# Gate columns projected first and row sums in two rounded parts, in the mixer of a two-layer trunk

## The chip, the core and the metric

One core of a Trainium2 chip runs the whole program. Its engines are TensorE (PE in the profile; PEld is its weight loading), VectorE (DVE), ScalarE (ACT), GpSimd (POOL) and SyncE (SP), each with its own instruction queue, ordered among each other by semaphores. The metric is the device time of one execution in microseconds, as the median of several runs.

## The reference, cut to what matters

Each of two layers adds a token mixer, a cross-attention and an expert retrieval to the residual stream. Only the front of the mixer is touched.

```python
def hybrid_mixer(h, w_in, conv_w, a_log, dt_bias, ...):     # h: 512 tokens x 1024
    proj = h @ w_in                                         # 1024 x 3600 columns
    gdn_qkv, gdn_gate, gdn_a, gdn_b, fox_qkv, fox_f = split(proj)
    gq, gk, gv = split(silu(causal_depthwise_conv(gdn_qkv, conv_w)))
    gq, gk = l2_norm(gq), l2_norm(gk)                       # 4 heads x 128
    log_alpha = -exp(a_log) * softplus(gdn_a + dt_bias)     # 4 columns
    beta = sigmoid(gdn_b)                                   # 4 columns
    o_gdn = gated_delta_rule(gq, gk, gv, log_alpha, beta)   # g = cumsum of log_alpha in chunks of 64
    fq, fk, fv = split(fox_qkv)
    fq, fk = rms_norm(fq), rms_norm(fk)                     # 8 heads x 64
    log_f = log_sigmoid(fox_f + fox_f_bias)                 # 8 columns
    o_fox = attention(fq, fk, fv, bias c_t - c_s, c = cumsum(log_f))
```

## The kernel before

Work is staged: at the end of a stage every compute engine drains and waits for the three others (`stage_end`). All times below are of layer 1; layer 2 runs the same code.

**Projection (S_PROJ).** A weight group is 512 columns of weights, 8 chunks of 128 rows of the contraction. For a product in full precision each operand is split into a rounded part (type fp32r) and the rest: ScalarE copies the rounded part (`w_hi` L868, `x_hi` L871), GpSimd subtracts for the weights (`w_lo` L1600), VectorE for the activations (`x_lo` L1226), and TensorE adds three products of parts (L451 to L453). A chunk of a group is so 4 tiles times 3 = 12 matmuls of 512 columns. `w_hi` and `w_lo` are rings of 4 chunks: ScalarE writes chunk c + 4 when TensorE has used chunk c, and writes the first 4 chunks (EARLY) of the next group before it stores the results of this one. Seven groups of 512 columns run (six for q, k, v, gate and the fox q and k, in a loop over pairs; one for fox v), then an eighth that has the 16 gate columns alone (16 moving columns, 96 matmuls). ScalarE stores each tile to `raw` (L905), VectorE convolves 12 of them (L1254, L1257), and at the end ScalarE applies SiLU to the gate (L914) and to the convolved tiles (L917).

**Norm factors (S_PREP).** VectorE forms 16 squares (L1215) into two buffers, TensorE sums each over its rows in plain fp32 (L493: `row_sums`), ScalarE makes the factors with Ln and Exp (L859, L861), TensorE spreads each row of factors over 128 partitions (L503: `spread_rows`), VectorE multiplies (L1291, L1293). The chain of the gate columns (L1263 to L1285 on VectorE, L921 to L925 on ScalarE) runs ahead of the squares.

**Cumulative sums (S_GATES).** TensorE forms them as columns and as rows (L534 to L542), ScalarE stores them and sends the fox rows to DRAM (`crow_dram`, L936); TensorE spreads the four other rows (L549) and ScalarE stores them to `gb` (L944).

Then S_KQ starts (L1302 on VectorE, L560 on TensorE). Much later, at the start of S_ONORM, one DMA reads `crow_dram` back to all partitions (`crow_all`, L974), for use in S_FOX (L1400).

## Time and profile before

| | us |
|---|---|
| median of 3 runs (4617.79 to 4626.66) | 4624.86 |
| the profiled execution | 4638.87 |
| its span | 4637.1 |
| layer 1: seven full groups of the projection, 29.2 to 191.4 | 162.2 |
| layer 1: from the end of the seventh group to the start of S_KQ, 191.4 to 296.9 | 105.5 |

The page gives the busy time of each engine, then the span in 40 slices, then DMA, then the chain of work that ended last. TensorE is 93% busy over the span, so a slice is worth looking at only where its digit or its clock (PEclk, tenths of full speed) is low. Each slice is 116 us. PEclk is 6 to 8 in slices 2 to 7 and in those that answer to them in layer 2, and 9 in nearly all others; the front of the mixer lies in slices 1 to 3.

### The profile page before, as it was taken

The numbers are of one execution on the slowest core, as the hardware profiler recorded it, in microseconds if no ns is written. First come the engines' busy times: TensorE is split into PE (matmuls) and PEld (weight loads), VectorE is DVE, ScalarE is ACT, GpSimd is POOL, SyncE is SP. The second block draws the span as 40 slices with busy tenths as digits, with TensorE's granted clock in tenths as the row PEclk, the third lists the DMA queues.
The fourth block names the chain that finished last, engine by engine and source line by source line (L and its number), as shares of the span: only waits on it lengthen the run. The fifth ranks groups of instructions, "written<-read, shape, count | busy, mean of one in ns | idle before, by whom it ended". The sixth has DMA issues, their size and how long they took to land.

```text
span 4637.1 us, 65551 instructions
## 1 busy us (share of the span) xinstructions
PE 4297.2 (93%) x20162; PEld 3507.6 (76%) x20162; DVE 2701.9 (58%) x5793; ACT 1534.5 (33%) x2429; POOL 1967.2 (42%) x1210
## 2 busy tenths in 40 slices
PE   7879888899999998999888798888999999989998
PEld 6648666688888887888776586666888888878886
DVE  5043523247586867888751426232566777778886
ACT  3311434333333333333333114343333232333333
POOL 4221132334343436777442311423343434367773
PEclk9867688999999999999998667889999999999999
DMA  3200021224353537999621001212243535379996
GB/s 121 87 1 1 35 76 63 91 79 144 125 200 122 204 119 286 343 336 341 228 110 73 1 1 46 81 55 84 93 143 120 205 119 207 135 284 341 336 335 226
DMA packets 218467, 695.21 MB, mean 150 GB/s; under 512 B 28224, under 2 KB 60992, under 8 KB 210128
## 3 DMA queue, kind: packets, MB, share of 16 engines
q1 hardware_dynamic: 132656, 448.94, 27.7%
q0 software_dynamic: 45888, 138.58, 7.8%
q10 hardware_dynamic: 39776, 105.86, 6.1%
q8 instruction: 76, 1.25, 0.1%
q14 instruction: 71, 0.58, 0.0%
HBM read 590.49 MB, written 102.79 MB: 150 GB/s over the span
## 4 chain that ended last, share of the span: by engine, by line
PE 64%; issue 23%; POOL 6%; DVE 3%; ACT 2%; DVEq 1%; ACTq 1%; POOLq 1%; DMA 0%
PE PS L451 16%; PE PS L452 16%; PE PS L453 16%; POOL u_lo L1663 6%; PE PS L503 2%; PE PS L812 1%; PE PS L493 1%; PE PS L632 1%; PE PS L633 1%; PE PS L597 1%; PE PS L583 1%; PE PS L727 1%; PE PS L627 1%; PE PS L622 1%; PE PS L660 1%
## 5 line engine op out<-in xcount | busy, mean ns | idle before, releaser
L1663 POOL TENSOR_TENSOR u_lo<-u_raw,u_hi 128x1024 fp32r<-128x1024 f32 x256 | 625.9, 2445 | 970.1 <-ACT u_hi L1084 970.1
L451 PE MATMUL PS<-h_hi,u_hi 128*128 128x512 f32 x2048 | 806.1, 394 | 3.0 <-POOL u_lo L1663 1.9
L452 PE MATMUL PS<-h_lo,u_hi 128*128 128x512 f32 x2048 | 797.3, 389 | 0.0
L453 PE MATMUL PS<-h_hi,u_lo 128*128 128x512 f32 x2048 | 797.2, 389 | 0.0
L1600 POOL TENSOR_TENSOR w_lo<-wring,w_hi 128x512 fp32r<-128x512 f32 (+1 forms) x352 | 459.6, 1310 | 621.7 <-ACT w_hi L868 618.7
L451 PE MATMUL PS<-v_hi,g_hi 128*128 128x512 f32 x1536 | 602.9, 392 | 24.4 <-DVE v_lo L1561 12.7
L452 PE MATMUL PS<-v_lo,g_hi 128*128 128x512 f32 x1536 | 601.7, 392 | 0.0
L453 PE MATMUL PS<-v_hi,g_lo 128*128 128x512 f32 x1536 | 601.4, 392 | 0.0
L1084 ACT ACTIVATE u_hi<-u_raw 128x1024 fp32r<-128x1024 f32 x256 | 271.0, 1060 | 948.4 <-PE PS L453 890.9
L1165 ACT ACTIVATE v_hi<-v_raw 128x1024 fp32r<-128x1024 f32 x256 | 271.5, 1061 | 575.5 <-PE PS L453 545.5
L1681 POOL DMA_INDIRECT v_row<-in_expert_v,row_index x256 | 382.3, 1493 | 167.9 <-DVE X L1567 110.3
L451 PEld LDWEIGHTS PS<-h_hi,u_hi 128*128 128x128 f32 x2048 | 384.9, 188 | 81.7 <-issue 5.1
L453 PEld LDWEIGHTS PS<-h_hi,u_lo 128*128 128x128 f32 x2048 | 384.4, 188 | 80.0
L452 PEld LDWEIGHTS PS<-h_lo,u_hi 128*128 128x128 f32 x2048 | 384.9, 188 | 76.2
L1675 POOL DMA_INDIRECT act<-acts_dram,act_index x256 | 394.2, 1540 | 108.0 <-issue 77.4
L868 ACT ACTIVATE w_hi<-wring 128x512 fp32r<-128x512 f32 (+1 forms) x352 | 215.2, 611 | 546.3 <-PE PS L453 479.1
L1567 DVE SCALAR_TENSOR_TENSOR X<-v_row,w,X 128x1024 f32<-128x1024 f32 x256 | 329.0, 1285 | 66.4 <-issue 50.9
L451 PEld LDWEIGHTS PS<-v_hi,g_hi 128*128 128x128 f32 x1536 | 291.1, 190 | 86.9 <-issue 26.3
L1561 DVE TENSOR_TENSOR v_lo<-v_raw,v_hi 128x1024 fp32r<-128x1024 f32 x256 | 313.4, 1224 | 72.2 <-ACT v_hi L1165 71.9
L452 PEld LDWEIGHTS PS<-v_lo,g_hi 128*128 128x128 f32 x1536 | 291.2, 190 | 60.5
L453 PEld LDWEIGHTS PS<-v_hi,g_lo 128*128 128x128 f32 x1536 | 290.8, 189 | 60.9
L1530 DVE TENSOR_SCALAR hot<-cst,pickT 128x128 f32<-128x128 f32 x384 | 221.9, 578 | 77.4 <-PE PS L812 47.4
(299 smaller groups left out, 7249.1 us busy)
## 6 DMA issues: line engine op xcount, KB each, us to landing
u_raw<-in_expert_u SPq DMA_DIRECT2D x256, 512.0 KB, 3.5
v_raw<-in_expert_v SPq DMA_DIRECT2D x256, 512.0 KB
wring<-in_weights SPq DMA_DIRECT2D x44, 2048.0 KB, 7.9
acts_dram<-act_ring ACTq DMA_DIRECT2D x256, 256.0 KB, 2.0
saved<-acts_dram SPq DMA_DIRECT2D x64, 768.0 KB
gates_dram<-gstage ACTq DMA_DIRECT2D x16, 2048.0 KB, 7.5
gates<-gates_dram SPq DMA_DIRECT2D x64, 512.0 KB
crow_all<-crow_dram ACTq DMA_DIRECT2D x2, 2048.0 KB, 8.4
```

The costliest lines, as they stand in the source:

```text
L451: mm(bank_ap, a_hi, b_hi, start=first, stop=False)
L452: mm(bank_ap, a_hi, b_lo, start=False, stop=False)
L453: return mm(bank_ap, a_lo, b_hi, start=False, stop=final)
L1084: fn(u_hi[:, slot, :], u_raw[:, slot, :], ACT.Copy).then_inc(uhi_ready, 1)
L1165: fn(v_hi[:, k % QUAD, :], v_raw[:, k % QUAD, :], ACT.Copy).then_inc(vhi_ready, 1)
L1530: v.tensor_scalar(hot(t, k)[:, 0, es], iota, hi_key, gate_col, ALU.is_equal, ALU.mult)
L1561: v.tensor_tensor(v_lo[:, k % QUAD, :], v_raw[:, k % QUAD, :], v_hi[:, k % QUAD, :].bitcast(f32), ALU.subtract).then_inc(vlo_ready, 1)
L1567: v.scalar_tensor_tensor(X[:, 0, :], v_rows[r][:], w0[:, bass.ds(g * PAIR + k, 1)], X[:, 0, :], ALU.mult, ALU.add).then_inc(macs_done, 1)
L1600: g.tensor_tensor(w_lo[:, c % WCHUNKS, 0:cols], wring[:, s, c, 0:cols], w_hi[:, c % WCHUNKS, 0:cols].bitcast(f32), ALU.subtract).then_inc( ...
L1663: g.tensor_tensor(u_lo[:, slot, :], u_raw[:, slot, :], u_hi[:, slot, :].bitcast(f32), ALU.subtract).then_inc(ulo_ready, 1)
L1675: g.indirect_dma_start(act0[:, k:k + 1], None, acts_by_place, bass.IndirectOffsetOnAxis(act_index[:, k:k + 1], 0)).then_inc(act_gathered[h ...
L1681: g.indirect_dma_start(v_rows[k % GATHERS][:], None, value_rows, bass.IndirectOffsetOnAxis(row_index[:, k:k + 1], 0)).then_inc(row_gathere ...
```

## The change

The stages S_PROJ, S_PREP and S_GATES become one, in this order of groups: first the 16 gate columns (group 0, now with the 16 weight columns stationary and 512 tokens moving), then the six groups of 512 columns (1 to 6), then fox v (group 7). The work of the other two stages is put between and into the groups.

- SyncE loads only the 16 columns for group 0 (pieces of 64 bytes).
- After group 1 TensorE turns the 16 rows into columns; VectorE's and ScalarE's gate chain follows beside groups 2 and 3.
- After group 3 TensorE forms the cumulative sums (4 products in place of 32) and waits until ScalarE has stored them; after group 4 one product turns them to rows, which go to DRAM, and TensorE waits until they have left PSUM.
- `gb` is read back from DRAM by four DMAs on ScalarE's queue, and `crow_all` by four DMAs, one for each 128 tokens, in pieces of 512 bytes instead of 2,048.
- The 16 squares are made twice: ScalarE's Square gives the rounded part, VectorE squares again and subtracts. TensorE sums both parts (32 fp32r matmuls instead of 16 fp32 ones, which the trace shows as two records each), three items behind each chunk of group 7.
- The factors are rounded into two parts as well, held in rows 0 to 23 and 32 to 55 of one tile, so that one fp32r matmul spreads an item.

```diff
+                for p in range(MIX_GROUPS):
+                    q, s = p // 2, p % 2
+                    if p >= 2:
+                        sp.wait_ge(w_free[s], l * N_PAIRS + (q + 1))
+                    if p == 0:
+                        sp.dma_start(wring[:, s, :, 0:16],
+                                     w_layer[PAIR_VS, 1].rearrange("p (c n) -> p c n", n=512)[:, :, 0:16]).then_inc(w_loaded[s], 16)
+                    else:
+                        sp.dma_start(wring[:, s].rearrange("p c n -> p (c n)"), w_layer[(p - 1) // 2, (p - 1) % 2]).then_inc(w_loaded[s], 16)
...
+                def small_product(c, m):
+                    return parts_product(PS[0:16, 7, :], w_hi[:, c % WCHUNKS, 0:16], w_lo[:, c % WCHUNKS, 0:16],
+                                         x_hi[:, c, :], x_lo[:, c, :], c == 0, c == DC - 1)
...
+                def mix_group(p, after_chunk=None):
+                    i0, b0 = 4 * (p - 1), 4 * ((p - 1) % 2)
+                    product = token_tile(0, (x_hi, x_lo), 512) if p == MIX_GROUPS - 1 else channel_tile(b0, (x_hi, x_lo), SEQ)
+                    weight_group(DC * p, 4, product, proj_done, free=lambda m: (raw_stored, i0 + m + 1), after_chunk=after_chunk)
...
+                def cumulative_sums():
+                    pe.wait_ge(gate_cols, 1)
+                    pe.wait_ge(raw_stored, 16)
+                    mm(PS[:, 7, 0:16], tri_chunk, la, start=True, stop=True)
+                    mm(PS[:, 7, 16:32], strict, la, start=True, stop=True)
+                    mm(PS[:, 7, 32:64], tri, lf, start=True, stop=False)
+                    mm(PS[:, 7, 32:64], ones, rinv[:], start=False, stop=True).then_inc(cums_done, 1)
+
+                def sums_to_rows():
+                    pe.wait_ge(cols_ready, 1)
+                    pe.wait_ge(raw_stored, 20)
+                    mm(PS[0:48, 3, 0:P], g_and_c, ident, start=True, stop=True).then_inc(rows_done, 1)
...
+                    pe.wait_ge(sq_hi_ready, i + 1)
+                    mm(PS[0:NROW2, 4, :], lhsT, sq_hi[:, i % 2, :], start=i == 0, stop=False)
+                    pe.wait_ge(sq_ready, i + 1)
+                    mm(PS[0:NROW2, 4, :], lhsT, sq_lo[:, i % 2, :], start=False, stop=i == N_QK - 1).then_inc(ss_done, 1)
+
+                def qk_row_sums(c):
+                    for i in range(3 * c, min(3 * c + 3, N_QK)):
+                        qk_row_sum(i)
+
+                weight_group(0, 1, small_product, small_done, x_chunk=lambda c: XP_MIX + c + 1)
+                mix_group(1)
+                small_to_columns()
+                pe.wait_ge(small_stored, 1)
+                mix_group(2)
+                mix_group(3)
+                cumulative_sums()
+                pe.wait_ge(cols_ready, 1)
+                mix_group(4)
+                sums_to_rows()
+                pe.wait_ge(rows_stored, 1)
+                mix_group(5)
+                mix_group(6)
+                mix_group(7, after_chunk=qk_row_sums)
+                pe.wait_ge(rs_ready, 1)
+                for i in range(N_QK):
+                    if i >= 4:
+                        pe.wait_ge(normed, i - 3)
+                    lhsT = sel_r[0:NROW2, i:i + 1].to_broadcast([NROW2, P]) if i < 8 else sel_pairs[0:NROW2, i - 8, :]
+                    mm(PS[:, 4 + i % 4, :], lhsT, rs_parts[0:NROW2, :], start=True, stop=True).then_inc(bc_done, 1)
```

```diff
+                def soft_exps():
+                    act.wait_ge(softarg, 1)
+                    fn(soft[:, :, :], soft[:, :, :], ACT.Exp, bias=zero_col, scale=-1.0)
+                    fn(nmax[:, 0:GH], par[:, PC["a_log"]:PC["a_log"] + GH], ACT.Exp)
+                    act.drain()
+                    fn(soft[:, :, 0:4], soft[:, :, 0:4], ACT.Ln, bias=1.0)
+                    fn(soft[:, :, 8:16], soft[:, :, 8:16], ACT.Ln, bias=1.0)
+                    act.drain().then_inc(softexp, 1)
...
+                def sums_store():
+                    act.wait_ge(cums_done, 1)
+                    fn(beg, PS[:, 7, 0:16], ACT.Exp)
+                    fn(esuf, PS[:, 7, 16:32], ACT.Exp)
+                    fn(gcol, PS[:, 7, 0:16], ACT.Copy)
+                    fn(ccol, PS[:, 7, 32:64], ACT.Copy)
+                    act.drain().then_inc(cols_ready, 1)
...
+                def qk_square(i):
+                    if i >= 2:
+                        act.wait_ge(ss_done, i - 1)
+                    fn(sq_hi[:, i % 2, :], conv[:, i, :] if i < 8 else raw[:, 8 + i, 3:RW], ACT.Square).then_inc(sq_hi_ready, 1)
+
+                split_first(l, 0, x_hi, hT, cols=16)
+                split_w(l, 0, 0, LATE, cols=16)
+                split_early(1)
+                act.wait_ge(small_done, 1)
+                fn(small_rows[0:16, :], PS[0:16, 7, :], ACT.Copy).then_inc(small_rows_stored, 1)
+                split_late(1)
+                split_early(2)
+                act.wait_ge(small_turned, 1)
+                fn(small.rearrange("p t n -> p (t n)"), PS[:, 7, 0:NT * 16], ACT.Copy).then_inc(small_stored, 1)
+                raw_store(1)
+                split_late(2)
+                split_early(3)
+                raw_store(2)
+                soft_exps()
+                split_late(3)
+                split_early(4)
+                raw_store(3)
+                sums_store()
+                split_late(4)
+                split_early(5)
+                rows_store()
+                raw_store(4)
+                split_late(5)
+                split_early(6)
+                raw_store(5)
+                conv_silu(0)
+                conv_silu(1)
+                act.drain().then_inc(qk_silu, 1)
+                split_late(6)
+                split_early(7)
+                raw_store(6)
+                fn(raw[:, 12:16, 3:RW], raw[:, 12:16, 3:RW], ACT.Silu)
+                conv_silu(2)
+                act.drain()
+                i = 0
+                for c in LATE:
+                    while i < 3 * (c - DC // 2) + 2:
+                        qk_square(i)
+                        i += 1
+                    split_w(l, (MIX_GROUPS - 1) // 2, (MIX_GROUPS - 1) % 2, [c])
+                for i in range(i, N_QK):
+                    qk_square(i)
+                act.wait_ge(ss_done, N_QK)
...
+                fn(rs_parts[0:NROW2, :], rs, ACT.Exp, bias=row_bias, scale=-0.5)
+                act.drain()
+                fn(rs, rs, ACT.Exp, bias=row_bias, scale=-0.5)
+                act.drain().then_inc(rows_ready, 1)
...
+                act.wait_ge(grow_saved, 16)
+                for t in range(NT):
+                    act.dma_start(gb[:, :, t * P:(t + 1) * P],
+                                  grow_dram[t * GH:(t + 1) * GH, :].rearrange("(o h) n -> o h n", o=1).to_broadcast([P, GH, P])).then_inc(gb_loaded, 16)
```

```diff
+                    if i >= 2:
+                        dve.wait_ge(ss_done, i - 1)
+                    v.tensor_tensor(sq_f[:, i % 2, :], x_i, x_i, ALU.mult)
+                    dve.drain()
+                    dve.wait_ge(sq_hi_ready, i + 1)
+                    v.tensor_tensor(sq_lo[:, i % 2, :], sq_f[:, i % 2, :], sq_hi[:, i % 2, :].bitcast(f32), ALU.subtract).then_inc(sq_ready, 1)
...
+                make_selectors()
+                dve.wait_ge(pad_zeroed, 1)
+                soft_arguments()
+                for m in range(4):
+                    convolve(m)
+                log_gates()
+                for m in range(4, 8):
+                    convolve(m)
                 dve.wait_ge(cols_ready, 1)
                 v.tensor_tensor(beg, beg, beta, ALU.mult)
-                stage_end(dve, l, S_GATES)
+                for m in range(8, 12):
+                    convolve(m)
+                for i in range(N_QK):
+                    square_low(i)
...
+                v.tensor_tensor(rs_parts[LOW_ROW:NROW2, :], rs_rows[LOW_ROW:NROW2, :], rs_parts[LOW_ROW:NROW2, :].bitcast(f32), ALU.subtract)
+                dve.drain().then_inc(rs_ready, 1)
+                for i in range(N_QK):
+                    dve.wait_ge(bc_done, i + 1)
+                    apply_qk(i, PS[:, 4 + i % 4, :])
+                stage_end(dve, l, S_PROJ)
```

What the order of instructions shows, at three places. On TensorE, between the end of the projection and the sums, before (`tmp` are the squares, `qk_t` the rows of factors, `stats` the gate columns):

```order
L453 MATMUL PS<-w_hi,x_lo 128x16
L493 MATMUL PS<-tmp,cst 24x512 [waits sq_ready,stage_done]
L493 MATMUL PS<-tmp,cst 24x512 [waits sq_ready] x15
L503 MATMUL PS<-qk_t,cst 128x512 [waits rs_ready]
L503 MATMUL PS<-qk_t,cst 128x512 x3
L503 MATMUL PS<-qk_t,cst 128x512 [waits normed] x4
```

and after, from the last matmul of the first chunk of group 7 on (L478 to L480 are the three products of parts; `sq_hi` and `sq_lo` the two parts of a square):

```order
L480 MATMUL PS<-w_hi,x_lo 128x512
L579 MATMUL PS<-sq_hi,row_r 56x512 [waits sq_hi_ready,raw_stored,selectors]
L581 MATMUL PS<-sq_lo,row_r 56x512 [waits sq_ready]
L579 MATMUL PS<-sq_hi,row_r 56x512 [waits sq_hi_ready]
L581 MATMUL PS<-sq_lo,row_r 56x512 [waits sq_ready]
L579 MATMUL PS<-sq_hi,row_r 56x512 [waits sq_hi_ready]
L581 MATMUL PS<-sq_lo,row_r 56x512 [waits sq_ready]
L478 MATMUL PS<-w_hi,x_hi 128x512 [waits w_lo_ready]
```

The sums stood behind the whole projection; now three items stand between two chunks of group 7, and the next chunk is queued behind them.

On TensorE, between groups 3 and 4, after (before, the next group followed at once, and these sums came after S_PREP):

```order
L480 MATMUL PS<-x_hi,w_lo 128x512
L562 MATMUL PS<-stats,cst 128x16 [waits raw_stored,gate_cols]
L563 MATMUL PS<-stats,cst 128x16
L564 MATMUL PS<-stats,cst 128x32
L565 MATMUL PS<-rinv,cst 128x32
L478 MATMUL PS<-x_hi,w_hi 128x512 [waits raw_stored,w_lo_ready,cols_ready]
```

The first matmul of group 4 now waits for `cols_ready`, which ScalarE gives when it has stored the sums.

On ScalarE, at the end of the projection, before (from the last early chunks of the 16-column group on):

```order
L868 ACTIVATE w_hi<-wring 128x16 [waits w_used] x3
L910 ACTIVATE fox_v<-PS 128x512 [waits proj_done] x4
L868 ACTIVATE w_hi<-wring 128x16 [waits w_used] x4
L913 ACTIVATE small<-PS 128x64 [waits proj_done]
L914 ACT_TABLE_LOAD
L914 ACTIVATE raw<-raw 128x4x512
L917 ACTIVATE conv<-conv 128x2048 [waits conv_done] x3
```

and after, from the last early chunks of group 7 on:

```order
L925 ACTIVATE w_hi<-wring 128x512 [waits w_used] x3
L963 ACTIVATE raw<-PS 128x512 [waits proj_done] x4
L1031 ACTIVATE raw<-raw 128x4x512
L993 ACTIVATE conv<-conv 128x2048 [waits conv_done]
L998 ACTIVATE sq_hi<-conv 128x512 x2
L925 ACTIVATE w_hi<-wring 128x512 [waits w_used]
L998 ACTIVATE sq_hi<-conv 128x512 [waits ss_done] x3
L925 ACTIVATE w_hi<-wring 128x512 [waits w_used]
```

The first squares stand behind four stores and two SiLUs of 2,048 columns, and the late weight chunks of group 7 stand behind squares.

## Rows read from the trace of the kernel before

**Rows 1.** The page: the span.

```profile
span 4637.1 us, 65551 instructions
```

**Rows 2.** Busy time by stretch (start:end, length, busy and count per engine, clock).

```profile
29.20:53.10 23.90, 23.80 (x96) 19.10 (x96) 8.43 (x7) 8.11 (x15) 14.23 (x10) 0.93 0.23 89
53.10:191.40 138.30, 135.11 (x576) 107.84 (x576) 47.27 (x48) 40.76 (x72) 62.23 (x48) 1.00 0.25 91
191.60:207.90 16.30, 16.24 (x96) 16.18 (x96) 0.00 (x0) 2.79 (x9) 1.09 (x5) 0.65 0.35 130
...
225.50:245.40 19.90, 17.06 (x32) 2.44 (x32) 10.13 (x15) 2.73 (x3) 0.00 (x0) 0.87 0.00 1
245.50:272.10 26.60, 25.77 (x48) 7.90 (x48) 11.49 (x16) 0.00 (x0) 0.00 (x0) 0.54 0.00 0
272.10:296.90 24.80, 22.45 (x72) 13.20 (x72) 0.17 (x1) 4.13 (x11) 0.00 (x0) 0.50 0.00 1
```

**Rows 3.** TensorE's timeline: start, duration; neighbours at half and full clock.

```profile
29.82 0.63 PE L452 MATMUL PS<-x_lo,w_hi 128*128 128x512 f32 x1
30.24 0.63 PE L453 MATMUL PS<-x_hi,w_lo 128*128 128x512 f32 x1
...
33.41 0.39 PE L453 MATMUL PS<-x_hi,w_lo 128*128 128x512 f32 x1
33.64 0.39 PE L451 MATMUL PS<-x_hi,w_hi 128*128 128x512 f32 x1
```

**Rows 4.** ScalarE's timeline: the end of the first group, and of the second.

```profile
53.11 0.63 ACT L868 ACTIVATE w_hi<-wring 128x512 fp32r<-128x512 f32 x1 [2.16 <-PEq L469]
53.65 2.04 ACT L905 ACTIVATE raw<-PS 128x512 f32 x4
...
75.90 0.63 ACT L868 ACTIVATE w_hi<-wring 128x512 fp32r<-128x512 f32 x1 [2.19 <-PEq L469]
```

**Rows 5.** Busy time in two stretches of the 16-column group: the clock (0.51).

```profile
191.40:196.40 5.00, 4.74 (x43) 4.77 (x43) 0.00 (x0) 2.69 (x8) 0.87 (x4) 1.00 0.01 3
196.40:201.00 4.60, 4.60 (x24) 4.60 (x23) 0.00 (x0) 0.22 (x1) 0.22 (x1) 0.51 0.38 89
```

**Rows 6.** TensorE's timeline in S_KQ: a start after an idle gap.

```profile
313.59 0.80 PE L560 MATMUL PS<-conv 128*128 128x128 f32 x2 [3.38 <-DVEq L1326]
```

**Rows 7.** ScalarE's timeline: the SiLUs, then the factors.

```profile
209.46 1.91 ACT L914 ACTIVATE raw<-raw 128x2048 f32<-128x2048 f32 x1
211.28 5.49 ACT L917 ACTIVATE conv<-conv 128x2048 f32<-128x2048 f32 x3
...
242.60 0.77 ACT L859 ACTIVATE qk_t<-PS,cst 24x512 f32<-24x512 f32 x1 [18.20 <-PE PS L493]
243.42 1.28 ACT L861 ACT_TABLE_LOAD   x1
244.72 0.72 ACT L861 ACTIVATE qk_t<-qk_t,cst 24x512 f32<-24x512 f32 x1
```

**Rows 8.** VectorE by tile or line: duration ns min/median/max, first and last start.

```profile
L1226 DVE TENSOR_TENSOR x_lo<-hT,x_hi x64: 677/1584/1786, 27.3 to 3118.6; 128x512 fp32r<-128x512 f32 x64
L1215 DVE TENSOR_TENSOR tmp<-conv x16: 684/692/693, 224.6 to 2540.8; 128x512 f32<-128x512 f32 x16
L1291 DVE TENSOR_TENSOR conv<-conv,PS x16: 686/687/690, 246.7 to 2564.7; 128x512 f32<-128x512 f32 x16
```

**Rows 9.** The page's costliest groups: GpSimd's subtraction for the weights.

```profile
L1600 POOL TENSOR_TENSOR w_lo<-wring,w_hi 128x512 fp32r<-128x512 f32 (+1 forms) x352 | 459.6, 1310 | 621.7 <-ACT w_hi L868 618.7
```

**Rows 10.** The tile crow_all: first use, issue of its DMA, time to landing.

```profile
L1400 DVE SCALAR_TENSOR_TENSOR tmp<-PS,stats,crow_all x64: 342/546/751, 497.5 to 2857.3; 128x128 f32<-128x128 f32 x16, 128x256 f32<-128x256 f32 x16, 128x384 f32<-128x384 f32 x16, 128x512 f32<-128x512 f32 x16
L974 ACTq DMA_DIRECT2D crow_all<-crow_dram x2: 351/354/356, 477.6 to 2784.9; - x2
...
DMA to landing us min/median/max: 8.3/8.4/8.4
```

**Rows 11.** Busy time by stretch in layer 2: 16-column group's end to S_KQ.

```profile
2515.20:2604.20 89.00, 65.30 (x154) 23.61 (x153) 24.71 (x49) 21.73 (x28) 0.00 (x0) 0.60 0.00 0
```

263 lines of the change are left out of this document (132 added, 131 removed).

## The prediction

> **What bounds the kernel now.** I read the page first: a span of 4637.1 us [rows 1] in which TensorE is busy 93%, so the gain must come from a stretch in which it is busy with little or slow. Then I cut layer 1 into stretches and read busy time and clock of each. The seven full groups run from 29.2 to 191.4 with 672 matmuls at full clock [rows 2]; two neighbours start 0.23 us apart, and 0.42 us at half clock [rows 3]. From 191.4 to 296.9, the start of S_KQ, lie 105.5 us without dense work: 16.3 for the 16 gate columns, 17.6 for SiLUs and the gate chain, 20 for the row sums, 26.6 for the spreading, 24.8 for the cumulative sums [rows 2]. Their clock is 0.50 to 0.65 but for the row sums. TensorE is "busy" there with tiny or two-pass fp32 products, and every engine waits for it or it for them, in turn. This stretch is on the path to the end, since S_KQ waits for all four engines. From the end of the 16-column group to S_KQ layer 1 has 89.0 us (207.9 to 296.9) and layer 2 has 89.0 too [rows 11], so the same sum holds for both.
>
> **The change part by part**, all for one layer against the 105.5 us that go.
>
> *Group 0.* 24 matmuls of 512 columns at 0.23 are 5.5 us; the old start of the first group at half clock moves from a full group to this one, so it costs about the same as before. The rounded and low parts of x, which the first group hid, now feed chunks of 0.7 to 1.3 us: x_lo takes 0.68 us when GpSimd rests and 1.58 beside GpSimd's subtraction [rows 8], and GpSimd has only 16 columns to subtract here. I take 5.7. Bounds: 5.5, and 10.2 if all 24 run at 0.42.
>
> *Boundaries.* The loop is unrolled. A boundary takes the first group's last early copy from 53.11 to the next at 75.90, 22.8 us [rows 4], while the mean is 138.3 / 6 = 23.05 [rows 2]. Six groups at 22.8: minus 1.5.
>
> *After group 1*: eight short records, then ScalarE must finish its early chunk and copy before group 2 starts; 1.2 us more than a boundary.
>
> *After group 3.* ScalarE's order is: early copy of group 4 (0.5), four stores (2.04) [rows 4], a table load (1.28) [rows 7], four short stores (0.4, my estimate), drain. TensorE waits for all of it, about 4.8 us after group 3 against the usual 0.6: plus 4.2. TensorE does eight tiny records and then idles some 3.5 us. The clock fell after 5 us of 16-column matmuls (0.51) [rows 5], and an idle gap of 3.38 us was followed by a start at half clock [rows 6], so I add one half-speed start, some ten matmuls at 0.2 more: 2.0. Behind this wait stands all of group 4; GpSimd and VectorE lose nothing. The page ScalarE: Activation LUTs, section on table sets, says that one set holds both exp and ln, so Exp after Ln needs no load. The trace shows a load of 1.28 us between Ln and Exp [rows 7]. By the rule the wait would be 1.3 us shorter; I go by the row.
>
> *After group 4*: one product, two short stores, drain: plus 1.0. The two DMA issues that follow (0.35 us each on ScalarE's queue, the price of the read in [rows 10]) are beside group 5.
>
> *Hidden work.* The gate chain stands between convolutions on VectorE, which is busy 47 of 138 us in the groups [rows 2]; Ln and Exp follow the stores of group 2 and have all of group 3. The SiLUs of q and k come after the stores of group 5: 0.3 + 0.5 + 2.04 + 1.28 + 3.7 = 7.8 us, then w_hi (0.5) and w_lo (1.3) [rows 9] of chunk 4: ready at 9.7, needed at 0.6 + 4 x 2.77 = 11.7. Slack 2.0 us; without it TensorE would wait by what is over.
>
> *Group 7.* This is the largest term. The first square stands on ScalarE behind the last early copy, four stores and two SiLUs of 1.85 [rows 7]: 0.3 + 0.5 + 2.04 + 1.85 + 1.85 + 0.1 + 0.6 = 7.3 us after group 6. TensorE has finished chunk 0 at 0.6 + 2.8 = 3.4 and waits at item 0. VectorE needs a product of 0.69, a drain of about 0.2 and a subtraction of 0.69 for each item [rows 8], 1.5 us, and only two buffers exist. Item 2 is summed at 11.3, and at 12.2 with GpSimd's subtraction beside it, which stretches a VectorE operation by 1.58 - 0.68 = 0.9 [rows 8]. From there a round is: chunk 2.8, two items ready 0.9, and the third, which VectorE may begin only when the first is summed: in all 5.2, and 5.9 with a stretch. Four rounds give 12.2 + 23.6 = 35.8, chunk 5 and item 15 38.5, chunks 6 and 7 44. TensorE is nearly idle for 8 us of it, so chunk 1 starts at half clock: plus 2.0. Together 46 us against 22.8: plus 23.2. Bounds: from below the 32 matmuls alone at 0.23, plus 7.3; from above no overlap of items with chunks, 4 + 16 x 2.1 + 22.8 = 60, with clock 62: plus 39. I take 23, since the waits are counted from rows.
>
> *Factors and spreading.* Ln 0.77, load 1.28, Exp 0.72 twice [rows 7] and a subtraction 0.69 are 4.4 us after item 15 (about 40.5), while chunks 6 and 7 run to 46: hidden by about 1 us. Then VectorE multiplies 16 items at 0.69 without waiting, for one spreading matmul takes 0.42 even at half clock: 11.0 plus 0.5 to start and end, 11.5. It was 26.6, since TensorE set the pace. `gb` is read meanwhile: ScalarE issues after the fox v copies, 3.5 us into the 11.5; 1 MB needs half of the 8.4 us of crow_all's 2 MB [rows 10]. Zero, at most 6.
>
> *crow_all* is issued 19.9 us ahead of its first use and lands in 8.4 [rows 10]: 11 us of slack for four times as many pieces. The three further issues (0.35 each) push ScalarE back by 1 us, of which 0.3 may show.
>
> Sum: 5.7 - 1.5 + 1.2 + 6.2 + 1.0 + 23.2 + 11.5 + 0.3 = 47.6. A layer gains 105.5 - 47.6 = 57.9, both 116. The profiled execution took 4638.9, 14 more than the median of 4624.9; 4638.9 - 116 = 4523, and for the median 4509.
>
> **The rivals.**
>
> *The squares fit beside the groups.* If ScalarE and VectorE keep ahead of TensorE (which the SiLUs ahead of them and the two buffers speak against), group 7 costs plus 9 instead of 23: 14 less a layer, 4481.
>
> *The items are slower than counted* (drains, semaphores and the half clock through all of group 7): near the upper bound, plus 37: 14 more a layer, 4537.
>
> *The short pieces are late.* If a piece of 512 bytes takes as long as one of 2,048, crow_all needs 33.6 us and S_FOX waits 14 us a layer; gb waits some 6. That is 4509 + 40 = 4549. No row has such pieces. The page DMA: Bandwidth & Descriptors (first table) gives 512 bytes as the least size for line rate; by that rule neither wait appears.
>
> *ScalarE starves TensorE.* Ahead of group 6's fifth chunk the slack is 2 us. If the queue is 5 us later than counted in groups 4 to 6, 3 to 6 us a layer are lost: about 4518.
>
> *Half clock through the projection; the slower end.* The new stretches of little activity are group 0, the sums after group 3 and the start of group 7. Each matmul at half clock costs 0.2 us, so from 290 of them a layer, three whole groups, the gain is gone; if the clock stayed low for all six groups (576 matmuls, 115 us a layer) the kernel would take 4509 + 230 = 4739. Against it: the first group rose to full clock within 4 us although it started cold [rows 2, 3]. [...]
>
> **How the numbers follow.** Forecast 4509: 0.60. Squares fit: 0.11. Slower items: 0.13. Short pieces: 0.07. Starving: 0.06. Half clock: 0.02. The remaining 0.01 is for no change. The forecast's own bounds are 4495 to 4523 (5 us a layer on group 7, 2 on the clock). The range reaches from the first rival to the short pieces: 4478 to 4549. About 0.2%, 9 us, is what a measurement of this kernel can tell from no change; faster by more 0.96, within 0.01, slower 0.03.
>
> **What would show it.** In the changed profile of layer 1: group 1 starts near 36.6; a gap of about 5 us after group 3 and no other above 2 us until group 6 ends near 181; then chunk 0 of group 7, TensorE waiting for ScalarE's square for 4 us, chunks 5 to 6 us apart, and 46 us in all; 16 multiplications on VectorE back to back in 11 us; S_KQ at about 238 instead of 297; the same in layer 2. S_FOX must start with no wait for crow_all. The prediction is wrong if group 7 takes under 35 or over 55 us, if gb or crow_all end a wait, or if the clock is 0.5 inside groups 2 to 6.

## The result and the profile after

The changed kernel takes **4513.56 us** (median of 4 runs, 4507.42 to 4518.06) against 4625.76 for the kernel before, timed beside it: a ratio of 0.9758, 95% interval 0.9739 to 0.9777. That is 112 us less. Forecast were 4509 and a gain of 116. The profiled execution took 4514.49 us; the page's first line of the changed kernel answers to [rows 1]:

```profile
span 4512.7 us, 64483 instructions
```

The best markers for the stages are ScalarE's early copies at the end of each weight group, as in [rows 4]: each of these was released by TensorE's queue at L498. Here is ScalarE's timeline of the changed kernel, layer 1 (start, duration, engine, line, tile, idle before and its releaser). Its first copy of x_hi starts at 25.97, before at 26.54.

```profile
57.79 0.63 ACT L925 ACTIVATE w_hi<-wring 128x512 fp32r<-128x512 f32 x1 [2.22 <-PEq L498]
81.92 0.63 ACT L925 ACTIVATE w_hi<-wring 128x512 fp32r<-128x512 f32 x1 [2.22 <-PEq L498]
104.61 0.63 ACT L925 ACTIVATE w_hi<-wring 128x512 fp32r<-128x512 f32 x1 [2.19 <-PEq L498]
133.29 0.63 ACT L925 ACTIVATE w_hi<-wring 128x512 fp32r<-128x512 f32 x1 [2.22 <-PEq L498]
156.93 0.63 ACT L925 ACTIVATE w_hi<-wring 128x512 fp32r<-128x512 f32 x1 [2.19 <-PEq L498]
179.83 0.63 ACT L925 ACTIVATE w_hi<-wring 128x512 fp32r<-128x512 f32 x1 [2.22 <-PEq L498]
```

The differences are 24.1, 22.7, 28.7, 23.6 and 22.9 us. Group 4 stands out with 28.7, and what surrounds it is in TensorE's timeline:

```profile
109.00 0.50 PE L478 MATMUL PS<-x_hi,w_hi 128*128 128x512 f32 x1 [3.16 <-ACTq L980]
...
109.64 0.63 PE L480 MATMUL PS<-x_hi,w_lo 128*128 128x512 f32 x1
110.07 0.63 PE L478 MATMUL PS<-x_hi,w_hi 128*128 128x512 f32 x1
...
112.98 0.40 PE L479 MATMUL PS<-x_lo,w_hi 128*128 128x512 f32 x1
113.22 0.39 PE L480 MATMUL PS<-x_hi,w_lo 128*128 128x512 f32 x1
```

TensorE waits 3.16 us for the sums' stores. Records 0.43 us apart are the half clock of [rows 3], and the full clock is back at 113. The first record alone (0.50) hides this; read the pitch of the next ones, or the granted clock of the stretch. Busy time by stretch, columns as in [rows 2]:

```profile
109.00:113.00 4.00, 4.00 (x11) 3.17 (x12) 3.70 (x7) 0.00 (x0) 0.00 (x0) 0.57 0.00 0
183.20:190.00 6.80, 1.36 (x4) 0.55 (x5) 3.19 (x4) 5.11 (x6) 1.33 (x1) 0.85 0.00 0
190.00:196.00 6.00, 5.73 (x16) 3.83 (x16) 3.58 (x6) 1.26 (x2) 0.00 (x0) 0.60 0.00 0
196.00:211.00 15.00, 10.58 (x42) 6.28 (x39) 11.71 (x14) 6.28 (x11) 4.88 (x3) 1.00 0.01 2
211.00:216.00 5.00, 4.60 (x13) 3.56 (x14) 2.94 (x5) 0.63 (x1) 0.00 (x0) 0.66 0.79 295
227.60:238.40 10.80, 8.16 (x16) 3.46 (x17) 10.14 (x16) 0.59 (x3) 0.00 (x0) 0.72 0.33 97
```

From 183 on this is group 7. TensorE's timeline there gives the waits at the row sums (L579 the rounded part, L581 the low part):

```profile
186.85 0.41 PE L579 MATMUL PS<-sq_hi,row_r 128*56 128x512 f32 x1 [3.84 <-ACT sq_hi L998]
...
189.76 0.67 PE L581 MATMUL PS<-sq_lo,row_r 128*56 128x512 f32 x1 [1.56 <-DVE sq_lo L1431]
...
197.26 0.44 PE L579 MATMUL PS<-sq_hi,row_r 128*56 128x512 f32 x1 [0.31 <-ACT sq_hi L998]
198.94 0.44 PE L581 MATMUL PS<-sq_lo,row_r 128*56 128x512 f32 x1 [1.25 <-DVE sq_lo L1431]
...
238.40 0.79 PE L617 MATMUL PS<-conv 128*128 128x128 f32 x2 [1.89 <-DVEq L371]
```

The first row sum, at 186.85, came after 3.84 us of waiting for ScalarE's square. S_KQ starts at 238.40 instead of 296.93. From the first copy of x_hi that is 212.4 us instead of 270.4: **58.0 us** gained in layer 1, where 57.9 had been forecast. In layer 2 the first copy of x_hi stands here on ScalarE's timeline, before and after:

```profile
2331.73 0.63 ACT L871 ACTIVATE x_hi<-hT 128x512 fp32r<-128x512 f32 x1 [18.20 <-DVEq L353]
```

```profile
2272.21 0.63 ACT L928 ACTIVATE x_hi<-hT 128x512 fp32r<-128x512 f32 x1 [18.97 <-DVEq L371]
```

S_KQ follows at 2604.20 [rows 11] and at 2484.25, so the stretch is 272.5 us before and 212.0 after: 60.4 us gained.

### The profile page after: what moved, and what is told of

Same layout as the page of the kernel before. It is cut to its first block, busy times and chain, and to the rows that moved or that the text cites. A ratio compares the mean times of both kernels' runs of the same rounds, so it can differ in the third digit from the quotient of the medians.

```text
span 4512.7 us, 64483 instructions
## 1 busy us (share of the span) xinstructions
PE 4180.8 (93%) x19846; PEld 3441.6 (76%) x19846; DVE 2726.2 (60%) x5857; ACT 1546.0 (34%) x2455; POOL 1962.0 (43%) x1210
## 4 chain that ended last, share of the span: by engine, by line
PE 70%; issue 13%; POOL 4%; DVE 4%; PEld 3%; ACT 3%; PEldq 1%; DVEq 1%; ACTq 1%; POOLq 1%; DMA 0%
PE PS L478 19%; PE PS L479 19%; PE PS L480 19%; POOL u_lo L1827 3%; PE PS L869 3%; PEld PS L478 1%; PEld PS L479 1%; PEld PS L480 1%; PEldq L498 1%; PE PS L689 1%; PE PS L690 1%; PE PS L640 1%; PE PS L654 1%; ACT junk L906 1%; PE PS L784 1%
## 5 line engine op out<-in xcount | busy, mean ns | idle before, releaser
L478 PE MATMUL PS<-h_hi,u_hi 128*128 128x512 f32 x2048 | 806.0, 394 | 3.4 <-ACT u_hi L1199 1.2
L480 PE MATMUL PS<-h_hi,u_lo 128*128 128x512 f32 x2048 | 797.2, 389 | 0.0
L478 PE MATMUL PS<-v_hi,g_hi 128*128 128x512 f32 x1536 | 602.3, 392 | 21.1 <-DVE g_lo L1723 21.1
L480 PE MATMUL PS<-v_hi,g_lo 128*128 128x512 f32 x1536 | 600.8, 391 | 0.0
L478 PEld LDWEIGHTS PS<-h_hi,u_hi 128*128 128x128 f32 x2048 | 384.9, 188 | 81.7 <-issue 5.0
L480 PEld LDWEIGHTS PS<-h_hi,u_lo 128*128 128x128 f32 x2048 | 384.4, 188 | 80.0
L478 PEld LDWEIGHTS PS<-v_hi,g_hi 128*128 128x128 f32 x1536 | 290.7, 189 | 83.5 <-ACT v_hi L1280 13.6
L480 PEld LDWEIGHTS PS<-v_hi,g_lo 128*128 128x128 f32 x1536 | 290.6, 189 | 61.0
L1696 DVE TENSOR_SCALAR hot<-cst,pickT 128x128 f32<-128x128 f32 x384 | 221.4, 577 | 77.5 <-PE PS L869 47.5
```

Source lines behind the costliest of these rows:

```text
L478: mm(bank_ap, a_hi, b_hi, start=first, stop=False)
L480: return mm(bank_ap, a_lo, b_hi, start=False, stop=final)
L1696: v.tensor_scalar(hot(t, k)[:, 0, es], iota, hi_key, gate_col, ALU.is_equal, ALU.mult)
```

## The experiments

All of them are edits of the changed kernel. The whole time differs by some us between runs of one kernel (the first below: 4497.2 to 4507.3), so I read each effect from the stretch that it touches: from the first 16-column product (27.58 in the changed kernel) to the start of S_KQ, by layer. The fourth column is the difference of the two layers' sum from the changed kernel's 421.3. The fifth is the tail of that stretch in each layer, from the last of ScalarE's early copies at the end of group 6 (179.83 and 2425.54 in the changed kernel) to the start of S_KQ.

| kernel | layer 1 | layer 2 | both, against changed | from group 6's end | median us |
|---|---|---|---|---|---|
| changed | 210.8 | 210.4 | | 58.6, 58.7 | 4513.56 |
| changed, run again | 212.7 | 210.7 | +2.1 | 58.9, 58.7 | 4515.53 |
| SiLUs spread | 207.3 | 207.0 | -7.0 | 54.7, 54.7 | 4497.36 |
| two sums a chunk | 206.1 | 206.6 | -8.6 | 53.6, 54.9 | 4497.74 |
| sums by tile | 198.0 | 198.5 | -24.8 | 44.6, 44.6 | 4483.94 |
| sums behind the group | 211.2 | 210.4 | +0.3 | 59.1, 59.1 | 4514.70 |
| sums' stores first | 206.2 | 206.9 | -8.2 | 58.3, 58.7 | 4505.56 |
| longer gap | 215.1 | 215.4 | +9.2 | 58.8, 58.8 | 4523.49 |
| no low part | 200.3 | 199.8 | -21.2 | 47.5, 47.5 | 4487.27 |
| fp32 spreading | 225.0 | 224.6 | +28.3 | 71.8, 71.8 | 4536.81 |
| combined | 192.3 | 193.3 | -35.7 | 44.6, 44.6 | 4481.04 |

Run again, the changed kernel's stretch is 1.9 us longer in layer 1 and 0.2 in layer 2, while its tail repeats within 0.3. What wanders ahead of the tail is the length of the stretches at half clock, in group 0 and at the start of group 4. So a difference of 2 us in the whole stretch can't be read, and for edits of group 7 the tail is the better measure.

My theory was the one of the prediction: in group 7 TensorE, ScalarE and VectorE take turns (a late first square, two buffers, VectorE's 1.5 us an item), and after group 3 TensorE waits for ScalarE's queue and loses its clock. The main rivals were that VectorE's pace alone sets group 7, and that the waits only show where something else ends.

### The first wait: SiLUs spread

```diff
-                fn(raw[:, 12:16, 3:RW], raw[:, 12:16, 3:RW], ACT.Silu)
-                conv_silu(2)
-                act.drain()
...
 # in qk_square(i), behind the square:
+                    if 4 <= i < 8:
+                        fn(raw[:, 8 + i, 3:RW], raw[:, 8 + i, 3:RW], ACT.Silu)
+                    elif 8 <= i < 12:
+                        act.wait_ge(conv_done, i + 1)
+                        fn(conv[:, i, :], conv[:, i, :], ACT.Silu)
```

> ScalarE's SiLUs of the gate rows and of the last four conv rows (1.93 us each, 182.28 to 186.0) are cut in eight pieces of one row and put behind squares 4 to 11, so that the first squares of the q/k items come right behind the stores of group 6. Theory A (the wait of 3.84 us behind chunk 0 of group 7 is the order of ScalarE's work and nothing else): the first row sum waits under 1 us, the rounds of later chunks stay at 5.9 to 6.2 us, S_KQ starts 3.3 us earlier in each layer, 4.7 us if chunk 1 (at half clock before, 191.6 to 194.6) now runs at full clock: 4504 to 4507 us. Rival B (VectorE's own 16 items of 1.5 us set the end of the group, and the first wait is only the place where it shows): the group ends within 1 us of where it did, 4512 to 4514. Rival C (the pieces now stand ahead of later squares): the third item of a chunk waits over 2 us instead of 1.3, 4513 to 4520.

TensorE's timeline: the first low part comes after 0.23 us, the later waits are as before, and the end moves with the start.

```profile
184.06 0.44 PE L581 MATMUL PS<-sq_lo,row_r 128*56 128x512 f32 x1 [0.23 <-DVE sq_lo L1433]
...
195.40 0.44 PE L581 MATMUL PS<-sq_lo,row_r 128*56 128x512 f32 x1 [1.24 <-DVE sq_lo L1433]
...
234.84 0.80 PE L617 MATMUL PS<-conv 128*128 128x128 f32 x2 [1.89 <-DVEq L371]
```

3.5 us a layer (3.9 and 4.0 in the tail), theory A. The median is 16 us down and lies below the expected 4504 to 4507; the stretch explains 7.0 of it, and the profiled execution took 4507.33. The half clock did not go with the first wait. Busy time by stretch shows it in chunk 1 and in chunk 3, with the full clock between:

```profile
188.00:192.40 4.40, 4.40 (x14) 3.40 (x13) 2.23 (x4) 1.15 (x2) 0.00 (x0) 0.61 0.00 0
192.40:202.00 9.60, 6.41 (x26) 3.72 (x25) 7.61 (x9) 6.58 (x12) 3.23 (x2) 1.00 0.00 1
202.00:206.20 4.20, 4.20 (x13) 3.26 (x12) 2.15 (x4) 1.15 (x2) 0.00 (x0) 0.59 0.01 4
```

So my prediction's reason for chunk 1's slow start (8 us in which TensorE is nearly idle) is not the whole of it: here the slow chunks stand behind waits of at most 1.61 us (chunk 1) and 1.33 (chunk 3). Why these are hit, and chunks 2 and 4, behind waits of 1.24 and 1.32, are not stays open. In the changed kernel the two slow chunks were 1 and 4; run again, its trace has 0.50 over 193 to 196 (chunk 1) and 0.64 over 208 to 212 (chunk 3). Which later chunk it hits wanders; that two of the eight are hit returned in both layers of all three traces.

### The third item's wait: two sums a chunk

```diff
-                    for i in range(3 * c, min(3 * c + 3, N_QK)):
+                    for i in range(2 * c, 2 * c + 2):
...
-                    while i < 3 * (c - DC // 2) + 2:
+                    while i < 2 * (c - DC // 2) + 2:
```

> Two row sums behind each of the eight chunks of group 7 instead of three behind the first five and one behind the sixth. Theory A (the third item of a chunk waits since there are two buffers, and VectorE needs 1.5 us for its part): no item waits but the first, rounds are 2.77 + 0.94 = 3.7 us instead of 5.9 to 6.2, group 7 takes 8 x 3.7 + 3.84 + 1.4 (chunk 1 at half clock) = 35 us instead of 47; but the factors (4.6 us from the last sum to the first spreading) now lie behind the group: S_KQ starts 6 to 8 us earlier in each layer, 4498 to 4502 us. Rival B (VectorE's pace of 1.5 us an item holds whatever stands between the items; with a subtraction of 1.60 beside GpSimd two items are 4.0 us): rounds of 4.0 us or more in the last chunks, 4501 to 4506. Rival C (the items wait for ScalarE's squares, which come one behind the other): rounds near 5, 4513 or more.

After the second item no row sum waits at all. TensorE's timeline has no gap between these lines of it, and 4.49 us at the factors, which now lie in the open:

```profile
190.04 0.67 PE L581 MATMUL PS<-sq_lo,row_r 128*56 128x512 f32 x1 [1.18 <-DVE sq_lo L1431]
...
222.65 4.15 PE L606 MATMUL PS<-rs_parts,sel_r 56*128 56x512 f32 x8 [4.49 <-DVEq L1460]
...
233.71 0.80 PE L617 MATMUL PS<-conv 128*128 128x128 f32 x2 [1.89 <-DVEq L371]
```

Busy time in most of the group:

```profile
197.00:218.00 21.00, 21.00 (x90) 14.95 (x88) 17.00 (x23) 8.22 (x13) 3.28 (x2) 1.00 0.27 101
```

That stretch is all work at full clock. The mechanism is theory A's, but the gain was 4.3 us a layer and not 6 to 8: the group took 38 us, not 35, since rounds were 3.7 to 3.9 and the one with a chunk at half clock 4.9 (190.51 to 195.40). The median fell by 16, of which the stretch explains 8.6; the rest lies outside it and is not shown to be an effect of the edit.

### Is anything hidden? Sums behind the group

```diff
-                mix_group(7, after_chunk=qk_row_sums)
+                mix_group(7)
+                for i in range(N_QK):
+                    qk_row_sum(i)
...
-                    while i < 3 * (c - DC // 2) + 2:
+                    while i < 2:
```

> All 16 row sums behind group 7 instead of between its chunks. Theory A (the rounds add up chunk and items rather than overlap them): group 7 takes 22.8 us as the other groups do, then 14 items at VectorE's 1.5 us and 4.6 us of factors, 49 to 50 us to the first spreading against 47.6: 1 to 3 us more in each layer, 4515 to 4520 us. Rival B (the chunks do hide the items): up to 16 x 1.5 = 24 us come into the open, 4540 to 4560.

TensorE's timeline, the first row sum, the last, and the spreading:

```profile
202.76 0.41 PE L579 MATMUL PS<-sq_hi,row_r 128*56 128x512 f32 x1 [0.26 <-issue]
...
222.75 0.68 PE L581 MATMUL PS<-sq_lo,row_r 128*56 128x512 f32 x1 [0.27 <-DVE sq_lo L1433]
227.92 4.15 PE L608 MATMUL PS<-rs_parts,sel_r 56*128 56x512 f32 x8 [4.50 <-DVEq L1462]
```

The group ran in 22.7 us, the sums behind it came one each 1.37 us from the third on, and the factors took 4.5 in the open. The end lies 0.2 us a layer from that of the changed kernel (0.4 to 0.5 in the tail), less than the 1 to 3 of theory A, and rival B is out. Putting the sums between the chunks, three at a time, hid none of the items' time: chunks and items added up. The equal ends are a balance all the same. Between the chunks the factors (4.5 us here in the open) are hidden, and the two chunks at half clock (3.1 us, none here) and the late first square take that back. The next run shows how much was still to be had.

### Truly overlapped: sums by tile

```diff
+SUM_TILE = [1 + 3 * i // 2 for i in range(N_QK)]
...
-                    if after_chunk is not None:
-                        after_chunk(c)
+                        if after_tile is not None:
+                            after_tile(4 * c + m)
...
+                qk_square(0)
+                qk_square(1)
                 raw_store(6)
...
-                    while i < 3 * (c - DC // 2) + 2:
+                    while i < sum(k <= 4 * (c - DC // 2) + 3 for k in SUM_TILE) + 2:
```

and the SiLUs in pieces, as above.

> The 16 row sums stand one by one behind single tiles of group 7 (behind tile 1 + 3i/2 of its 32: two sums for every three tiles, the last behind tile 23), the first two squares stand ahead of group 6's stores, and the SiLUs are in pieces as in the kernel with the spread SiLUs. Theory A (TensorE and VectorE took turns: two items' work ahead is all that two buffers allow while a whole chunk runs, so 16 items of 1.5 us and 22.2 us of chunks added up to 47): TensorE's 24 tiles and 16 sums are 24 x 0.69 + 16 x 0.47 = 24.1 us, VectorE's 16 items 24 to 27.6 us (four subtractions at 1.60), so the last sum is done 26 to 29 us after group 6, and chunks 6 and 7 (5.5 us) hide the factors: the group takes 31 to 35 us instead of 47.2, 12 to 16 us less in each layer, 4481 to 4490 us. Rival B (each item costs the chain square, subtraction, row sum, whose latency two buffers don't hide): a period of 1.9 us or more, the last sum at 32 or later, 4492 to 4500. Rival C (only the first wait goes, as with the spread SiLUs): 4505.

TensorE's timeline, then busy time by stretch:

```profile
195.13 0.44 PE L582 MATMUL PS<-sq_lo,row_r 128*56 128x512 f32 x1 [0.17 <-DVE sq_lo L1437]
...
202.64 0.44 PE L582 MATMUL PS<-sq_lo,row_r 128*56 128x512 f32 x1 [0.91 <-DVE sq_lo L1437]
...
214.78 3.85 PE L608 MATMUL PS<-rs_parts,sel_r 56*128 56x512 f32 x8
...
225.55 0.80 PE L619 MATMUL PS<-conv 128*128 128x128 f32 x2 [1.89 <-DVEq L372]
```

```profile
180.00:190.00 10.00, 8.73 (x35) 5.49 (x35) 7.53 (x10) 7.35 (x14) 2.77 (x3) 1.00 0.00 0
190.00:197.00 7.00, 6.83 (x30) 4.72 (x29) 6.70 (x10) 5.62 (x11) 1.72 (x1) 1.00 0.00 1
197.00:212.00 15.00, 13.96 (x60) 9.96 (x59) 11.22 (x15) 9.42 (x14) 3.27 (x2) 1.00 0.39 141
```

The longest wait left is 0.91 us, VectorE is busy 14.2 of the 17 us up to 197, and the clock stays at 1.00. The gain is 12.9 and 11.9 us by layer over the whole stretch: theory A. In the tail it is 14.0 and 14.1; the difference was lost ahead of the edited part, where group 0 and the start of group 4 stayed at half clock longer in this execution.

### The price of the low part

```diff
-                    pe.wait_ge(sq_ready, i + 1)
-                    mm(PS[0:NROW2, 4, :], lhsT, sq_lo[:, i % 2, :], start=False, stop=i == N_QK - 1).then_inc(ss_done, 1)
...
-                for i in range(N_QK):
-                    square_low(i)
```

> The low rounded part of the squares is left out (16 products and subtractions on VectorE, 16 row sums on TensorE), so the sums are of squares rounded once. Theory A (the waits behind the items are VectorE's part, 7.5 us in all: 1.56, 0.27, 1.25, 1.32, 1.30, 1.33, 0.46): they go, and 16 row sums of 0.23 (3.8 us) with them; the first wait of 3.8 us for ScalarE's square stays: group 7 is 11 us shorter in each layer, 4489 to 4493 us; since item 15 still ends behind chunk 5, the factors stay hidden. Rival B (the third item of a chunk waits for ScalarE's square, as the rows with 0.30 before L579 say of their first half): its wait stays above 0.8 us and only the row sums and some of the waits go, 4498 to 4506.

TensorE's timeline, at a third item:

```profile
194.70 0.44 PE L579 MATMUL PS<-sq_hi,row_r 128*56 128x512 f32 x1 [0.78 <-ACT sq_hi L996]
```

10.6 us a layer (11.1 and 11.2 in the tail) against 11 expected, though the expectation lists a wait too many: the changed kernel's layer 1 has no second 1.30, and its six waits for VectorE's part add up to 6.2 us. But the third item still waits 0.78 us for ScalarE's square, which VectorE's longer part had covered. With two buffers both engines start the third item late, and the wait is what the slower one leaves.

### After group 3: the stores first, and a longer gap

```diff
-                raw_store(3)
                 sums_store()
+                raw_store(3)
```

> ScalarE stores the cumulative sums ahead of group 3's four raw stores instead of behind them. In the changed kernel TensorE waits 3.16 us after the sums (105.83 to 109.00), of which the stores are 2.04 and a table load 1.28; the load can start at 105.2 as soon as ScalarE has no stores ahead of it. Theory A (my step on the gap: TensorE waits for all that stands ahead on ScalarE): the load ends at 106.5, four short stores and a drain at 107.1, group 4 starts at 107.2 to 107.4: 1.7 us less in each layer, 4509 to 4511 us. Rival B (the table load hides in neither case and the stores were beside it): group 4 starts within 0.5 us of 109.0, 4513.

The gap, on two engines:

```profile
105.03 1.28 ACT L976 ACT_TABLE_LOAD   x1
106.33 0.18 ACT L976 ACTIVATE stats<-PS 128x16 f32<-128x16 f32 x1
```

```profile
106.83 0.50 PE L478 MATMUL PS<-x_hi,w_hi 128*128 128x512 f32 x1 [1.22 <-ACTq L980]
107.17 0.39 PE L479 MATMUL PS<-x_lo,w_hi 128*128 128x512 f32 x1
```

The first fence is ScalarE's timeline, the second TensorE's. The gap shrank by 1.94 us (1.7 expected), but the gain was 4.1 a layer, twice that: after 1.22 us of idling group 4 started at full clock, in both layers. From early copy to early copy group 4 took 25.0 us instead of 28.7 and 28.3. I had missed it in writing the expectation, since I had read only the first record after the changed kernel's gap and taken its start for a fast one. The other half of the test has six more copies of a bank ahead of the stores:

```diff
+                    for i in range(6):
+                        fn(sq_f[:, i % 2, :], PS[:, i % 4, :], ACT.Copy)
+                        act.drain()
```

> Six copies of a bank (0.62 us each and a drain, into a buffer that nothing reads) stand ahead of the storing of the cumulative sums, so TensorE's gap after group 3 grows from 3.16 to some 7 to 7.6 us, 4.0 to 4.4 more in each layer. Theory A (the step of my prediction that failed: an idle gap of this kind is followed by a start at half clock, only that 3.16 us out of a dense group weren't enough): group 4's first ten matmuls or more are 0.43 apart, 2 us or more on top: 4525 to 4530 us. Rival B (one gap, however it is doubled, between dense groups costs only itself): group 4 starts 0.23 apart, 4521 to 4523.

TensorE's timeline of this kernel:

```profile
112.85 0.80 PE L478 MATMUL PS<-x_hi,w_hi 128*128 128x512 f32 x1 [7.02 <-ACTq L983]
113.44 0.63 PE L479 MATMUL PS<-x_lo,w_hi 128*128 128x512 f32 x1
...
117.55 0.39 PE L480 MATMUL PS<-x_hi,w_lo 128*128 128x512 f32 x1
```

Both theories of this text start from my misreading, so neither stands as written. Group 4 starts at half clock with a gap of 3.16 and with one of 7.02. TensorE is back at full clock 4.0 us after the first and 4.4 after the second, so the longer gap costs little more than itself: 3.86 of the 4.6 a layer measured. The length of the slow start wanders more than that by itself: after the same gap of 3.1 to 3.2 us it was 3.5 to 6.1 us in the two layers of the eight traces that have it, and after 7.02 it was 4.4 and 4.9. So these runs show no growth with the gap. After 1.22 us there was no slow start; nothing between 1.22 and 3.1 was run.

### The spreading in one fp32 part

```diff
-                    lhsT = sel_r[0:NROW2, i:i + 1].to_broadcast([NROW2, P]) if i < 8 else sel_pairs[0:NROW2, i - 8, :]
-                    mm(PS[:, 4 + i % 4, :], lhsT, rs_parts[0:NROW2, :], start=True, stop=True).then_inc(bc_done, 1)
+                    for half, lhsT in enumerate(heads_of):
+                        last = mm(PS[half * part:(half + 1) * part, 4 + i % 4, :], lhsT, rs_rows[0:NROW, :], start=True, stop=True)
+                    last.then_inc(bc_done, 1)
```

> The 16 factors are spread from one unrounded fp32 row set of 24 rows, by 24 matmuls in two passes as in the kernel before, instead of by 16 matmuls over 56 rows in two rounded parts; all else is as changed. Theory A (the spreading fell from 26.6 to 10.8 us because TensorE set its pace before and VectorE's multiplication does now): 48 records of 0.54 at half clock, 25.8 us, VectorE waits before each multiplication, 15 us more in each layer, 4541 to 4546 us. Rival B (the spreading was slow before only by its clock, and follows the groups here at full speed): 48 records of about 0.27 are 13 us, 2 to 4 us more in each layer, 4518 to 4522.

VectorE's timeline, and busy time by stretch:

```profile
233.26 0.69 DVE L1439 TENSOR_TENSOR conv<-conv,PS 128x512 f32<-128x512 f32 x1 [0.17 <-PE PS L608]
234.39 0.69 DVE L1439 TENSOR_TENSOR conv<-conv,PS 128x512 f32<-128x512 f32 x1 [0.44 <-PE PS L608]
236.10 0.69 DVE L1439 TENSOR_TENSOR conv<-conv,PS 128x512 f32<-128x512 f32 x1 [1.02 <-PE PS L608]
```

```profile
228.60:233.50 4.90, 4.82 (x12) 2.14 (x12) 2.98 (x5) 0.61 (x2) 0.00 (x0) 1.00 0.65 190
233.50:252.50 19.00, 18.11 (x38) 4.70 (x36) 8.49 (x12) 0.01 (x1) 0.00 (x0) 0.51 0.02 6
```

The first five items ran at full clock, 0.86 apart, and even then VectorE waited 0.17 for each; from 234 the clock is 0.51, although TensorE is busy 95% of the stretch, and items come 1.71 apart. 14.2 us a layer (13.1 to 13.3 in the tail): near theory A's 15, with a piece of B in the first five. Most of it is the clock: at the pace of those five, 16 items would take 13.8 us (an estimate), 3.7 more than the changed kernel's 10.1. What brought the clock down, the 24 rows or the two passes, was not separated.

### Everything together

By tile, stores first, and one more line behind `split_late(3)`:

```diff
+                fn(nmax[:, 31:32], zero_col, ACT.Exp)
```

> Three edits together on the changed kernel: the row sums one by one behind single tiles of group 7 with the early squares and the SiLUs in pieces; the sums' short stores ahead of group 3's four raw stores; and one Exp of a single column behind ScalarE's late copies for group 3, where it idles 2.1 us before each copy, so that the table for the sums' Exp is already loaded (1.28 us that TensorE waits for at present). Theory A (the three gains lie on different stretches and add): 4484 of the by-tile kernel, less 8 for the stores and the clock that stays up after group 3, less 1.2 in each layer for the load: 4472 to 4476 us. Rival B (TensorE's clock after group 3 is not a matter of the gap alone, and the gain of 8 was half luck of one kernel): 4477 to 4482. Rival C (the extra Exp stalls a weight copy, or its table is pushed out again by a later function before it is used): the load still stands before L976's operations and 4475 to 4480 comes out.

> The changed kernel itself, beside the combined one on the same chip, as the base of its comparison: 4511 to 4517 us by both theories. Its trace tells whether the two stretches of half clock in group 7 (chunk 1 and chunk 4) and the one after group 3 belong to the program (Theory A: they return at the same chunks within one) or wander by chance (Rival B: other chunks, or none).

TensorE's timeline of the combined kernel, at the start of group 4:

```profile
106.84 0.50 PE L479 MATMUL PS<-x_hi,w_hi 128*128 128x512 f32 x1 [0.54 <-ACTq L982]
107.17 0.40 PE L480 MATMUL PS<-x_lo,w_hi 128*128 128x512 f32 x1
```

The load is gone from the gap (0.54 instead of 1.22). S_KQ starts at 220.26, and the stretch is 35.7 us shorter over both layers than the changed kernel's. The gains add: the tail is 14.0 and 14.1 us shorter, as in the by-tile kernel, and group 4 takes 24.1 us instead of 28.7 and 28.3. That is 36.9, of which group 0 and group 1 gave back 1.4 in layer 2, by a longer start at half clock. Without the load the gap is 0.68 us shorter, not 1.2 as expected. The time is 4481.04 us (4474.53 to 4482.68), ratio to before 0.9680 (0.9666 to 0.9693), beside 4515.53 and 0.9758 (0.9744 to 0.9771) for the changed kernel beside it on the same chip. That is 34.5 us less than the changed kernel, and 5 more than my 4472 to 4476. The median falls into rival B's range, but neither rival's mechanism is in the trace: group 4 started at full clock in both layers, and the load is gone. The rest of the program (span less both stretches) is 4091.5 us in the changed kernel, 4094.2 here, and between 4084 and 4092 in the other traces; whether it answers to the edits or wanders by itself stays open. Against the by-tile kernel the medians are only 3 apart, so the gain of the two further edits rests on the stretches. Of the repeated changed kernel, theory A's chunks came back within one, as told above.

## Why the prediction was right, step by step

Predicted and measured for one layer, in us:

| step | predicted | measured, and from where |
|---|---|---|
| group 0 and group 1, against the old first group | +5.7 | +5.25: (57.79 - 25.97) - (53.11 - 26.54) [rows 4] |
| group 2 with the turning before it | 24.0 | 24.1 |
| group 3 | 22.8 | 22.7 |
| group 4: gap 4.2 and slow start 2.0 | 29.0 | 28.7: gap 3.16 after the sums, half clock to 112.9 |
| group 5 with the rows before it | 23.8 | 23.6 |
| group 6 | 22.8 | 22.9 |
| group 7 | 46 | 47.5: 179.83 to the last matmul's end near 227.4 |
| factors and spreading behind it | 11.5 + 0.3 | 11.0 |
| the whole, against the same stretch before | -57.9 | -58.0 |

That the total is right to 0.1 us is luck: group 7 took 1.5 us more than forecast, and the first step 0.5, group 4 0.3 and the work behind group 7 0.8 less. The steps are the better test, and none is off by more than 1.5. Layer 2, which I had taken as equal on the strength of the part behind the 16-column group [rows 11], gained 60.4: ahead of that part the kernel before took 2.1 us longer there than in layer 1, and the changed kernel 0.4 less. Group 1 started at 35.07 and not near 36.6; the first product came 1.6 us after the first copy of x_hi, instead of 2.7 before.

*Group 7* was the largest term and right in its parts: TensorE waited 3.84 us at item 0 (4 expected), the first square was ready 7.2 us after the end of group 6 (7.3), and a round at full clock took 6.2 (5.9), with the one stretched subtraction that I had counted. The term came out 1.5 us too small: 1.1 of it is the clock, since I had one slow chunk for 2.0 us and there were two, for 1.5 and 1.6 (4.25 and 4.35 us instead of 2.77); the rest is in the rounds. What I had not seen is that this layout gains nothing over a plain sequence (sums behind the group: 0.2 to 0.5 us a layer more). My lower rival, squares that fit beside the groups, did not come, and the by-tile kernel shows what it would have needed: an order in which VectorE is never without an item. It gains 14.0 and 14.1 from the end of group 6 on, against the 14 of that rival.

*After group 3*: the wait, its parts (four stores, a load of 1.28, four short stores) and the slow start were all there. The rule of the Trainium skill, page ScalarE: Activation LUTs (section on table sets: ln and exp share a set), did not hold here either: L1046's Exp, behind L1044's Ln, stands behind a load of 1.28 us at 222.84, and L976's Exp, the next after L970's Ln, behind another at 107.20. An Exp as the last function loaded does serve the next Exp, as the combined kernel shows.

*Hidden work*: no wait of TensorE above 2 us stood between 35 and 180 but the one after group 3, so the starving of group 6 did not come. The factors ended at 226.4 and chunk 7 at 227.4: hidden by 1 us, as counted (the prediction's terms for the factors add up to 4.2 us, not to its 4.4). 16 multiplications took 10.1 us (11.0), since back to back they run 0.61 to 0.67 apart and not 0.69: a small miss.

*Short pieces*: gb's four reads land within 4.4 us of their issue, the last issued by 229.7, and are first used at 238.5. crow_all's land in 4.0 to 7.3 us, and the first use comes 22.2 us after the first issue. From the start of S_KQ to it are 200.5 us, and 200.6 before. Neither is waited for; the 0.3 that I gave to the later issues was not there either.

*The clock through the projection*: 1.00 over the 46 us of groups 2 and 3 and of 5 and 6. Half clock took 4.0 us after group 3 and two chunks of group 7. One of my signs of being wrong, a clock of 0.5 inside groups 2 to 6, contradicts my own term for group 4: it asked for the absence of the slow start that the sum counts with 2.0 us.

*The sum and the time*: 58.0 and 60.4 are 118.4, and the medians differ by 112. The interval of the ratio is worth 9 us either way, so the 6 between them can't be read. The profiled spans differ by 124.4, of which 6.0 lie outside the changed stretches. The profiled execution of the kernel before was 14 us above its median; that the 6.0 are its own is not shown by any run. Of the chances, the 0.03 for slower is 0.01 more than its one rival has.

## What to carry to other kernels

Work put between the chunks of a matmul stream is hidden only if its slowest engine has an item in hand the whole time. With two buffers that engine can do only two items' work while a chunk runs, however many are summed behind it. Three at a time cost as much here as all of them behind the group; one at a time, at the pace of the slowest engine, took 14 us less in each layer. Test the hiding by moving the work behind the stream: if the time stays, nothing was gained by the interleaving.

Where TensorE waits for a small result, let the engine that delivers it do that first and the bulky stores after, with its function table loaded in advance. Here the clock made a wait of 3.2 us cost about 5, and one of 1.2 cost only itself.

Read more than one record after a gap before saying at which clock the engine started.
